# A two-layer hybrid block: where token sums, branch products and expert loads stand in the order of each engine

## The chip, the cores and the metric
One core of a Trainium2 chip runs one launch of the kernel. Five engines take their instructions in their own order: TensorE (PE), VectorE (DVE), ScalarE (ACT), GpSimd (POOL) and SyncE (SP), which here only issues transfers. They meet through semaphores, and 16 DMA engines move data between HBM and SBUF. The metric is the device time of one launch in microseconds (us), the median of the runs.

## The reference, cut to what matters
Per layer, for 128 prompt tokens and 512 sample tokens (640 rows of width 1024, all float32):
```python
h = modulate(rms_norm(x, norm1_g[l]), sh1, sc1)      # sh, sc, g: adaLN, silu(cond) @ w_mod[l] + b_mod[l]
u_f, q_g, k_g, v_g, q_d, k_d, v_d, gates = split(h @ w_in[l])     # q_g and k_g normalised, rope on sample tokens
o_g = gqa_attention(q_g, k_g, v_g)                   # 8 heads, 2 kv heads
o_d = diff_attention(q_d, k_d, v_d, diff_lambda[l], ...)          # 4 heads, softmax minus lambda * softmax
g_f, g_g, g_d = split(sigmoid(gates), 3)
merged = g_f * (fourier_mix(u_f) @ w_f) + g_g * (o_g @ w_go) + g_d * (o_d @ w_do)
x = x + g1 * (merged @ w_out[l])
h = modulate(rms_norm(x, norm2_g[l]), sh2, sc2)
x = x + g2 * moe(h, ...)     # 16 experts in 4 groups, 2 of the best group for each token
```
There are two layers; a last rms_norm gives the outputs, and the new keys and values are returned too.

## The kernel before, in words
**Precision.** A float32 product is made of three fast ones: each operand is split into a high part, rounded by a copy, and a low part, the difference. `mm_split` (matmuls at L181) does high x high, high x low and low x high. So every 1 MB chunk of weights needs a high part from ACT (`hi`, L897) and a low part from POOL (`lo`, L817) or DVE (`first_lo`, L1220; L1299) before TensorE can use it. Activations lie with features on partitions: `x_T`, `h_hi`, `h_lo`, 8 blocks of 128 features by 640 tokens.

**Start of layer 1.** SP loads four 2 MB blocks of the modulation weights and the first two chunks of w_in (`stream`, L720). TensorE turns x to `x_T`, does the modulation products (`mod_product(0..3)`, L1594), spreads the norm's factors over the partitions (`spread_rstd`), turns the gains (`row_in`) and the modulation (`turn_mod`, L1583). DVE copies the norm's factors, computes the low part of the first weights (L1220, 27.47), the first scaled block, the gains, and the multiplier `mul1`; then ACT modulates (L151), DVE and POOL split `h` (L163, L166, L174), and TensorE begins with the first chunk's products (`project`, L181). Its second half of features waits for modulation blocks 2 and 3. When its first modulations are done ACT issues eight small loads (L212 to L214, L908 to L912), the last of them `lam_in`, from diff_lambda (L912). DVE's next step (L1274) needs it, and behind that on DVE stand the folded inputs of the Fourier part (L1290 to L1293) that TensorE reads at L1698.

**Projections.** SP loads the DFT tables, rope and caches, then chunk after chunk into two buffers (`raw`, `stream(i)`). Behind `stream(4)` it stores `x_T` to HBM (`x_kept`, L752), since its room is used later; semaphore `x_moved` tells POOL. TensorE does for each chunk five token tiles ("z" units) and turns the normed and roped tiles back ("x" units). Four PSUM banks go round; ACT empties them (L1016, L1034) and DVE does norm and rope (L1335 to L1374).

**Token sums.** The gate and merge products use fewer multiplications through sums of blocks (a Strassen-like scheme): four token-side sums s_1 to s_4 of `h`, and weight-side sums of blocks of each chunk (`block_sum`, L1481, on DVE; `block_hi`, L1060, on ACT; `block_lo`, L874, on POOL, all 128x512). In the order of POOL, five token-wide adds (L833, 128x1280) stand behind its last low part of a chunk, so they run at the start of the attention. ACT makes the high parts (`sum_high(0)`, `sum_high(1)`, L1047) at items 12 and 13 of the attention, and POOL then the low ones (L855). The third sum follows the attention: three adds, then `sum_high(2)` on ACT ahead of the block parts, and POOL's low part (L863). DVE adds up the fourth (L1488 to L1491) after the first block sums.

**Attention.** `att` lists the items, one head of one token tile each. For each: scores (L1684), maximum (L1380), exponential (L977), division (L1392, DVE), turning and values (L1776). In layer 1 TensorE also does the rest of the modulation products; in layer 2 gate products.

**Merge.** The branch products (`branch(n)`, with `pw_hi` and `pw_lo`, L1096 and L1452) and the remaining gates in blocks (L1509 adds their parts), then the output products with w_out. Counter `g_pfree` counts the branch weights that are used up, and `o_full` (1 to 8) the finished output blocks. In layer 2 the program's order is branch(0), branch(1), branch(2), ... with the blocks between them, and DVE's first block sums come before `mg_sum` (L1536) of the first branch.

**MoE.** SP issues four expert loads of 512 KB (L1974) at `g_pfree` 24, and the other twenty of the first tile (L1980, L1966) once all output products are done and the last low part of the weights is read. The router's result is worked out on DVE (L2171 to L2316). DVE makes `h_tok` (L2186), and POOL scatters the token rows to HBM in the order of experts with ten indirect transfers (L2034). SP waits for all of them, then loads the sorted rows (`h_sel`, L1988), then issues the loads of the next tile (L1957, L1961). TensorE gathers the first tile's rows by products (L2451), does the first tile (L2422) and turns the next rows (L2410).

## Time and profile before

| | |
|---|---|
| median of 3 runs (lowest, highest) | 1942.72 us (1937.16, 1942.76) |
| profiled execution; its span | 1943.26 us; 1941.2 us |
| busy: PE, DVE, ACT, POOL | 1726.5, 957.3, 718.6, 501.9 us |
| mean granted TensorE clock | 0.957 |
| layer 1: start and projections, attention, merge, MoE | to 217, 400, 709, 990 us |
| layer 2: the same | to 1185, 1349, 1650, 1941 us |

The stage ends are read from the timelines. "Busy" counts the time in which an engine executes; a granted clock of 1.00 is 2.4 GHz and of 0.50 is 1.2 GHz. In a timeline's row stand the start, the length, the engine, the line of the program and the tiles written and read; in brackets stands how long the engine was idle before, and what released it. A queue is q1 for SP's and q10 for ACT's transfers, q0 for POOL's.

### The profile page before, as it was taken

What the parts mean: (1) busy time and instruction counts of PE and PEld (TensorE: products, weight loads), DVE (VectorE), ACT (ScalarE), POOL (GpSimd) and SP (SyncE); (2) the same over time, 40 slices, a digit from 0 to 9 for tenths busy, and PEclk for the clock granted to TensorE, in tenths of its full rate; (3) what the DMA queues carried; (4) which work ended last, traced back from release to release, by engine and by line L of the source; (5) the groups of instructions that cost most, each with busy time, mean ns of one, the idle gap of its engine ahead of it and who ended that gap; (6) DMA issues with size and microseconds to landing.
All of it is one profiled execution on the core that took longest, in us unless ns stands there. A gap on an engine that the chain in (4) does not pass through costs nothing. (4 is left out here: it accounts for less than half of the span.)

```text
span 1941.2 us, 34689 instructions
## 1 busy us (share of the span) xinstructions
PE 1726.5 (89%) x13363; PEld 1351.5 (70%) x13363; DVE 957.3 (49%) x1849; ACT 718.6 (37%) x1394; POOL 501.9 (26%) x268
## 2 busy tenths in 40 slices
PE   5999999989999987788689998888899999588893
PEld 4899866679999974222188997567899998432222
DVE  4285476785667333111283744766766652611114
ACT  4443465553433421111254434656433342211113
POOL 1303410065456302000101123201545551200004
PEclk8999999999999988999789999999999999899996
DMA  7512377823522337987442221001232340889744
GB/s 275 195 44 68 106 249 248 275 94 129 192 91 88 143 143 298 360 303 261 143 147 98 67 67 36 1 2 44 66 98 66 98 145 21 354 311 393 278 136 174
DMA packets 170647, 305.95 MB, mean 158 GB/s; under 512 B 12530, under 2 KB 123250, under 8 KB 169716
## 3 DMA queue, kind: packets, MB, share of 16 engines
q1 hardware_dynamic: 151248, 249.09, 37.1%
q10 hardware_dynamic: 13476, 33.67, 4.8%
q0 software_dynamic: 5760, 20.97, 2.9%
q8 instruction: 107, 1.75, 0.4%
q14 instruction: 56, 0.46, 0.1%
HBM read 517.87 MB, written 41.68 MB: 288 GB/s over the span
## 5 line engine op out<-in xcount | busy, mean ns | idle before, releaser
L2422 PE MATMUL psum<-xw,h_T 128*32 128x512 f32 x1792 | 209.3, 611 | 36.0 <-DMA xw<-w_expert 32.4
L181 PE MATMUL psum<-whi,h_hi 128*128 128x256 f32 x720 | 210.1, 292 | 0.5 <-ACT v_tok L1011 0.5
L817 POOL TENSOR_TENSOR wlo<-raw,whi 128x2048 fp32r<-128x2048 f32 x25 | 115.2, 4608 | 362.3 <-ACT whi L897 362.3
L181 PE MATMUL psum<-whi,h_lo 128*128 128x256 f32 x720 | 203.5, 283 | 0.0
L181 PE MATMUL psum<-wlo,h_hi 128*128 128x256 f32 x720 | 203.5, 283 | 0.0
L2422 PEld LDWEIGHTS psum<-xw,h_T 128*32 128x32 f32 x1792 | 53.9, 111 | 170.5 <-issue 113.5
L977 ACT ACTIVATE prob<-psum,small_stats 128x640 f32<-128x640 f32 (+1 forms) x160 | 112.0, 705 | 134.5 <-DVE small_stats L1380 134.3
L1380 DVE TENSOR_REDUCE small_stats<-psum 128x1 f32<-128x640 f32 (+1 forms) x160 | 107.3, 712 | 96.7 <-PE psum L1684 72.2
L2319 DVE TENSOR_TENSOR gated_x<-psum,sig_x 128x256 f32<-128x256 f32 x28 | 11.9, 425 | 279.9 <-ACT sig_x L2066 279.9
L181 PEld LDWEIGHTS psum<-whi,h_hi 128*128 128x128 f32 x720 | 137.5, 191 | 3.0 <-issue 1.8
L181 PEld LDWEIGHTS psum<-wlo,h_hi 128*128 128x128 f32 x720 | 137.9, 192 | 0.0
L181 PEld LDWEIGHTS psum<-whi,h_lo 128*128 128x128 f32 x720 | 137.6, 191 | 0.0
L874 POOL TENSOR_TENSOR weight_block_lo<-weight_block_sum,weight_block_hi 128x512 fp32r<-128x512 f32 x84 | 116.3, 1416 | 79.8 <-DVE weight_block_sum L1481 63.3
L2041 POOL DMA_INDIRECT y_ab<-y_rows,rows_ab x20 | 23.0, 1150 | 431.4 <-DMA y_rows<-y_sel 425.9
L2435 PE MATMUL psum<-xw,act_T 128*32 128x512 f32 x896 | 110.7, 630 | 21.2 <-DMA xw<-w_expert 11.5
L874 POOL TENSOR_TENSOR weight_block_lo<-raw,weight_block_hi 128x512 fp32r<-128x512 f32 x63 | 105.2, 1683 | 74.1 <-ACT weight_block_hi L1060 74.1
L181 PE MATMUL psum<-h_hi,weight_block_hi 128*128 128x320 f32 x336 | 103.8, 309 | 0.0
L181 PE MATMUL psum<-h_lo,weight_block_hi 128*128 128x320 f32 x336 | 103.8, 309 | 0.0
L181 PE MATMUL psum<-h_hi,weight_block_lo 128*128 128x320 f32 x336 | 103.8, 309 | 0.0
L1684 PE MATMUL psum<-k_T,q_T 64*128 64x320 f32 x512 | 86.2, 455 | 14.8 <-ACT prob L977 14.2
L2435 PEld LDWEIGHTS psum<-xw,act_T 128*32 128x32 f32 x896 | 29.0, 115 | 96.5 <-issue 69.7
L181 PE MATMUL psum<-branch_hi,pw_hi 128*128 128x320 f32 x384 | 88.9, 313 | 4.6 <-DVE pw_lo L1452 4.6
(375 smaller groups left out, 4108.3 us busy)
## 6 DMA issues: line engine op xcount, KB each, us to landing
xw<-w_expert SPq DMA_DIRECT2D x672, 512.0 KB
raw<-w_in SPq DMA_DIRECT2D x46, 1024.0 KB, 5.4
wm_rest<-w_mod SPq DMA_DIRECT2D x40, 1024.0 KB, 5.3
y_rows<-y_sel ACTq DMA_DIRECT2D x108, 128.0 KB, 5.2
h_sel<-h_rows ACTq DMA_DIRECT2D x22, 512.0 KB, 6.9
wm<-w_mod SPq DMA_DIRECT2D x4, 2048.0 KB, 16.1
raw<-w_out SPq DMA_DIRECT2D x8, 1024.0 KB, 5.2
h_rows<-c_zero ACTq DMA_DIRECT2D x4, 1536.0 KB, 8.9
```

Source lines behind the costliest of these rows:

```text
L181: mm = pe.matmul(dst, st, mv[q], start=start and n == 0, stop=stop and n == 2)
L817: pool.tensor_tensor(wlo[i % 2][:, :, :], raw[i % 2][:, :, :], whi[i % 2][:, :, :].bitcast(F32), ALU.subtract).then_inc(w_lo, 1)
L874: pool.tensor_tensor(dst, src, w_ring[0][:, slot, :, :].bitcast(F32), ALU.subtract).then_inc(w_lo, 1)
L977: act.activation(dst, scores_view(i, m), ACT.Exp, bias=small[:, s, 0:1], accum_out=small[:, s, 1:2]).then_inc(t_exp, 1)
L1380: dve.tensor_reduce(small[:, 2 * (i % 3) + m, 0:1], scores_view(i, m), AX.X if att[i][2] == 0 else AX.XY, ALU.max, negate=True).then_inc(t ...
L1684: mm = pe.matmul(pair(m)[:, hf, 0:HALF], q_slice(i, m), k_slice(i, m, hf * HALF, (hf + 1) * HALF), start=True, stop=True)
L2041: pool.indirect_dma_start(out=y_ab[t][:, s, :], out_offset=None, in_=y_rows, in_offset=bass.IndirectOffsetOnAxis(ap=pos_ab[:, s, t:t + 1], ...
L2319: dve.tensor_tensor(gated_x[:, :], psum[:, i % 2, 0:DE], sig_x[:, :], ALU.mult).then_inc(x_gt, 1)
L2422: mm = pe.matmul(psum[list_rows(q), i % 2, :], hT[i % 2][:, kc, q, :], xw[q][c][:, k * 512:(k + 1) * 512], start=(kc == 0), stop=(kc == KD ...
L2435: mm = pe.matmul(psum[list_rows(q), 5 + hf, :], aT[i % 2][:, j, list_rows(q)], xw[q][N_PARTS + hf][:, j * 512:(j + 1) * 512], start=(j == ...
```

## The change
It moves steps within the orders of the engines; the mathematics and the matmuls stay.
- Start of layer 1: the spread norm and the turned gains come before `mod_product(1)`; the low part of chunk 0 comes behind `mul1` on DVE; ACT's high part of chunk 1 comes behind the first modulation; `mod_product` and `turn_mod` of blocks 2 and 3 take other places between the projections.
- `x_kept` is stored behind `stream(2)`, in both layers.
- POOL's five adds come behind its low part of chunk 3, and the low parts of s_1 and s_2 behind that of chunk 6; ACT's high parts of both come before two z units of chunk 5.
- Merge of layer 1: `sum_high(2)` comes behind the first two block parts. Layer 2: POOL's third sum waits for the end of the turned differential outputs, `sum_high(2)` comes behind all seven block parts, DVE's first block sums behind `mg_sum` of the second branch, and s_4's low part behind the fourth.
- MoE: seven expert loads instead of four at `g_pfree` 24, four more at `o_full` 6, and the others as before.
```diff
-                        if i == 4:
+                        if i == 2:
                             if first:
                                 sp.wait_ge(s_xe, KD)
                             sp.dma_start(x_kept, x_T[:, :, :]).then_inc(x_moved, 16)
...
                         lo(i)
+                        if i == CH_KVG - 1:
+                            first_sums()
+                        if i == CH_QD + 1:
+                            for n, s in enumerate((s_1, s_2)):
+                                pool.wait_ge(a_hi, n + 1)
+                                pool.tensor_tensor(s[1], (f_1, f_2)[n][1], f32(s[0]), ALU.subtract).then_inc(a_lo, 1)
+
+                    if not first:
+                        pool.wait_ge(d_3, DH)
                     pool.wait_ge(t_o, NA)
...
-                        hi(1)
...
                             modulate_act(act, h_mix, mul1, shift1, kc)
+                        if first and kc == 0:
+                            hi(1)
...
+                        if u in (("z", CH_QD, 1), ("z", CH_QD, 3)):
+                            sum_high(u[2] // 2)
...
-                        if i in (12, 13):
-                            sum_high(i - 12)
...
-                        sum_high(2)
                         pw_high(1)
                     else:
                         pw_high(0)
-                        sum_high(2)
...
                     keep_diff()
-                    for j in range(2, 7):
-                        block_hi(n0, j)
+                    if first:
+                        sum_high(2)
+                        for j in range(2, 7):
+                            block_hi(n0, j)
+                    else:
+                        for j in range(2, 7):
+                            block_hi(n0, j)
+                        sum_high(2)
...
-                        first_lo(dve, 0)
...
                         scaled_gain(mul1, 8, 0, 0, 4).then_inc(m_done, 1)
-                    else:
-                        pass
+                        first_lo(dve, 0)
...
-                            if g == 0:
+                            if not first and g == 1:
+                                first_blocks()
+                            if g == (0 if first else 3):
                                 dve.wait_ge(a_hi, 4)
...
                         mod_product(0)
-                        mod_product(1)
                         spread_rstd(pe)
                         pe.wait_ge(s_row, 16 * 3 * DEPTH)
                         pe.transpose(psum[:, 4, 0:P], row_in[:, :], ident[:, :]).then_inc(m_rt, 1)
+                        mod_product(1)
...
-                            if kc < 2:
-                                mod_product(2 + kc)
-                            if 1 <= kc < 3:
-                                turn_mod(1 + kc)
+                            if kc % 2 == 0:
+                                mod_product(2 + kc // 2)
+                            else:
+                                turn_mod(2 + kc // 2)
...
                     sp.wait_ge(g_pfree, 24)
-                    for c in range(N_PARTS):
-                        sp.dma_start(xw[0][c][:, :], w_exp[c, 0]).then_inc(xw_ld[c], 16)
+                    EARLY = [(c, 0) for c in range(N_PARTS + 1)] + [(2, 3), (3, 3)]
+                    LAST_STREAM = [(0, 2), (1, 2), (2, 1), (3, 1)]
+                    for c, q in EARLY:
+                        first_part(c, q)
+                    sp.wait_ge(o_full, KD - 2)
+                    for c, q in LAST_STREAM:
+                        first_part(c, q)
                     sp.wait_ge(o_full, KD)
```
`first_sums` holds the five adds of L833 with the waits that they had (`n_lo`, `x_moved`), `first_blocks` the block sums and the three steps of s_4 (L1488 to L1491), and `first_part(c, q)` one expert load of 512 KB. Behind the last line the loads of the first tile that are in neither list follow.

## Rows read from the trace of the kernel before

**Rows 1.** The page, part 4: the chain that ended last, by line.
```profile
PE psum L181 22%; SPq L1957 2%; PE psum L1684 2%; DMA xw<-w_expert 2%; ACT prob L977 2%; PE psum L2422 1%; PE psum L2435 1%; DVE small_stats L1380 1%; SPq L1961 1%; SPq L1953 1%; PE psum L1716 1%; PE psum L1749 1%; DVE prob L1392 1%; POOL h_rows L2034 1%; PE psum L1776 0%
```

**Rows 2.** Timeline of DVE in layer 1's start: start, us, what, [idle before <-releaser].
```profile
27.47 2.29 DVE L1220 TENSOR_TENSOR wlo<-raw,whi 128x2048 fp32r<-128x2048 f32 x1 [0.80 <-ACT whi L897]
...
67.60 0.29 DVE L1274 TENSOR_TENSOR lam_pr<-lam_in 128x128 f32<-128x128 f32 x1 [9.95 <-DMA lam_in<-diff_lambda]
...
97.05 0.42 DVE L1335 TENSOR_REDUCE z_ss<-z_q 128x4 f32<-128x256 f32 x1 [22.79 <-ACT z_q L1022]
```

**Rows 3.** Timeline of TensorE in layer 1's start.
```profile
34.07 0.87 PE L181 MATMUL psum<-h_hi,whi 128*128 128x320 f32 x2 [6.54 <-DVE h_lo L166]
...
70.57 0.67 PE L1698 MATMUL psum<-dft_ch,u_T 128*128 128x256 f32 x2 [0.27 <-DVE u_middle L1293]
```

**Rows 4.** Timeline of the issuing queues, ACT's and SP's, in layer 1's start.
```profile
60.47 0.86 ACTq L912 DMA_DIRECT2D lam_in<-diff_lambda  x1
...
56.10 1.40 SPq L720 DMA_DIRECT2D raw<-w_in  x2
```

**Rows 5.** DMA views of 63.5 to 67 (second line: queue) and 87 to 92.
```profile
q10 hardware_dynamic: 517, 0.15, 18.9%
...
DMA packets 122, 2.14 MB, mean 429 GB/s; under 512 B 4, under 2 KB 18, under 8 KB 18
```

**Rows 6.** Windows of five attention items: us, busy (x) by engine, PEclk, DMA share, GB/s.
```profile
1203.30:1227.19 23.89, 17.95 (x165) 13.06 (x163) 20.16 (x30) 12.23 (x26) 15.70 (x6) 0.93 0.01 1
1247.83:1267.60 19.77, 16.53 (x164) 12.04 (x162) 12.80 (x30) 12.22 (x26) 0.00 (x0) 1.00 0.00 1
247.78:269.30 21.52, 21.39 (x246) 14.13 (x242) 14.53 (x35) 12.29 (x25) 0.00 (x0) 1.00 0.76 244
269.30:291.70 22.40, 21.91 (x251) 14.65 (x247) 17.15 (x36) 14.54 (x27) 5.83 (x2) 1.00 0.74 243
```

**Rows 7.** Timeline of POOL, in layer 1's projections and layer 2's attention.
```profile
82.05 4.52 POOL L817 TENSOR_TENSOR wlo<-raw,whi 128x2048 fp32r<-128x2048 f32 x1 [0.91 <-ACT whi L897]
...
1210.15 2.89 POOL L833 TENSOR_TENSOR h_sum_second_f<-h_sum_second_f,h_sum_first_f 128x1280 f32<-128x1280 f32 x1
```

**Rows 8.** Timeline of DVE in layer 2's attention.
```profile
1211.92 4.56 DVE L1392 TENSOR_SCALAR prob<-prob,small_stats 128x640 f32<-128x640 f32 x2
...
1224.65 1.02 DVE L1392 TENSOR_SCALAR prob<-prob,small_stats 128x640 f32<-128x640 f32 x2
```

**Rows 9.** Window in layer 1's projections; columns as in rows 6.
```profile
108.00:124.00 16.00, 16.00 (x137) 16.00 (x136) 13.59 (x39) 8.21 (x23) 0.00 (x0) 1.00 0.22 68
```

**Rows 10.** Timeline of ACT, in layer 1's projections and merge.
```profile
127.65 0.36 ACT L1034 ACTIVATE q_T<-psum 128x256 f32<-128x256 f32 x1
...
412.28 1.26 ACT L1047 ACTIVATE h_sum_hi<-h_sum_second_f 128x1280 fp32r<-128x1280 f32 x1
```

**Rows 11.** Timeline of TensorE: projections, MoE of layer 1, merge and MoE of layer 2.
```profile
129.42 0.36 PE L181 MATMUL psum<-whi,h_hi 128*128 128x256 f32 x1
...
755.90 1.97 PE L2410 MATMUL psum<-ident,h_sel 128*128 128x128 f32 x8 [5.62 <-DMA h_sel<-h_rows]
...
1380.78 0.90 PE L181 MATMUL psum<-branch_hi,pw_hi 128*128 128x320 f32 x2 [4.60 <-DVE pw_lo L1452]
...
1697.35 1.97 PE L2410 MATMUL psum<-ident,h_sel 128*128 128x128 f32 x8 [5.95 <-DMA h_sel<-h_rows]
```

**Rows 12.** Windows: the lower clock in layer 2's merge, and the output products.
```profile
1379.90:1386.70 6.80, 5.92 (x22) 5.92 (x23) 4.04 (x3) 0.86 (x1) 4.44 (x2) 0.50 0.17 31
1606.00:1650.00 44.00, 44.00 (x297) 38.38 (x295) 10.03 (x22) 8.32 (x14) 5.80 (x2) 1.00 0.00 1
```

**Rows 13.** DMA queues from 1672 to 1694: packets, MB, share of 16 engines.
```profile
q0 software_dynamic: 1440, 5.24, 58.5%
q1 hardware_dynamic: 792, 2.85, 32.3%
```

**Rows 14.** The chain that ended last, 1640 to 1760, in order of time.
```profile
1684.96 8.55 DMA h_rows<-h_tok,rows_ab
```

More of the change, by code:

```diff
@@ L822, in _ @@
                             modulate_pool(pool, h_mix, kc)
-                    for i in range(2, N_WIN + n0):
-                        if i in (CH_KVG, CH_QD):
-                            continue
-                        lo(i)
                     n_step = [0]
@@ L1481, in block_sum, with first_blocks @@
                         dve.tensor_tensor(out, x, y, ALU.subtract).then_inc(q_sum, 1)
-                    for m in range(4):
-                        block_sum(n0, m)
-                    dve.wait_ge(a_step, SUM_STEPS)
                     s4_hi, s4_lo = f_4
-                    dve.wait_ge(a_lo, 2)
-                    dve.tensor_tensor(s4_lo, h_12[0].bitcast(F32), s_2[0].bitcast(F32), ALU.subtract).then_inc(a_step, 1)
-                    dve.tensor_tensor(s4_hi, h_12[1].bitcast(F32), s_2[1].bitcast(F32), ALU.subtract).then_inc(a_step, 1)
-                    dve.wait_ge(a_step, SUM_STEPS + 2)
-                    dve.tensor_tensor(s4_lo, s4_lo, s4_hi, ALU.add).then_inc(a_step, 1)
+                    def first_blocks():
+                        for m in range(4):
+                            block_sum(n0, m)
+                        dve.wait_ge(a_step, SUM_STEPS)
+                        dve.wait_ge(a_lo, 2)
+                        dve.tensor_tensor(s4_lo, h_12[0].bitcast(F32), s_2[0].bitcast(F32), ALU.subtract).then_inc(a_step, 1)
+                        dve.tensor_tensor(s4_hi, h_12[1].bitcast(F32), s_2[1].bitcast(F32), ALU.subtract).then_inc(a_step, 1)
+                        dve.wait_ge(a_step, SUM_STEPS + 2)
+                        dve.tensor_tensor(s4_lo, s4_lo, s4_hi, ALU.add).then_inc(a_step, 1)
+                    if first:
+                        first_blocks()
                     n_acc = 0
@@ L1962, in load_down @@
                                      bounds_check="skip_entire_dma").then_inc(xd_ld[h], 16)
-                    def first_down(q):
-                        for h in range(2):
-                            sp.dma_start(xw[q][N_PARTS + h][:, :], w_exp[N_PARTS + h, PER_LIST * q]).then_inc(xd_ld[h], 16)
                     def store_y(i, lists):
@@ L1977, in _ @@
                     low_ready(sp, N_STREAM - 1)
-                    for c in range(N_PARTS):
-                        for q in range(1, N_LISTS):
-                            sp.dma_start(xw[q][c][:, :], w_exp[c, PER_LIST * q]).then_inc(xw_ld[c], 16)
-                    for q in (0, 1, 3):
-                        first_down(q)
+                    rest = [(c, q) for c in range(N_PARTS) for q in range(N_LISTS)] + [(N_PARTS + h, q) for q in (0, 1, 3) for h in range(2)]
+                    for c, q in rest:
+                        if (c, q) not in EARLY + LAST_STREAM:
+                            first_part(c, q)
                     sp.wait_ge(k_d, TT)
-                    first_down(2)
+                    for h in range(2):
+                        first_part(N_PARTS + h, 2)
                     sp.wait_ge(k_t, KD)
```

42 lines of the change are left out of this document (22 added, 20 removed).

## The prediction
> **What bounds the kernel now.** I read the chain that ended last first [rows 1]: by line, the split products of TensorE (L181) hold the largest part, and two causes stand in the MoE, the loads of expert weights and POOL's scatter of the token rows (L2034). So TensorE's own time is the floor nearly everywhere, and the change moves no matmul away: it can gain only where TensorE waits or where the clock is down, and it loses wherever a moved step makes TensorE wait. I then took the six places that the diff touches, one by one, in the timelines of their engines and in windows. All times are of the profiled execution, 1943.26 us around a span of 1941.2; the median of the three runs is 0.5 lower, so I subtract the same gain from 1942.72.
>
> **1. Start of layer 1.** DVE's low part of the first weights, 2.29 us at 27.47 [rows 2], stands ahead of the gains and the first scaled rows; behind it comes the row that ends TensorE's wait of 6.54 us at 34.07 [rows 3]. Taken out of that path it gives some 2.0 us, as the spread norm and the turned gains come before the second product of the modulation vector. But what TensorE reaches next is not its own to start early: at 70.57 it waits for DVE [rows 3], and DVE stands at 67.60 after 9.95 us of waiting for the load of diff_lambda [rows 2], which ACT issues at 60.47, behind its scalings [rows 4]. ACT's last scalings are released by the last mod turn, which with the new order I put 0.25 us later, not sooner, so the 2.0 us are spent in front of 70.57. I take +0.3 us (0 to 1; it would be -2.0 if the load were already there, and the row says it is not).
>
> **2. The store of x_T (L752) is issued behind stream 2 instead of stream 4.** Nothing on an engine waits for it but POOL's sums. It does lie in SP's queue in front of stream 3 and beside ACT's small loads. Stream 2 (issued in the pair at 56.10 [rows 4]) is through near 63.5, and at that point 517 packets of the ACT queue are still to come [rows 5]: about 32 for each of 16 engines. Now the store follows. Its packets show from 87 to 92: 122 packets make 2.14 MB, 20 KB for nearly every one, at 429 GB/s [rows 5]; the 2.6 MB of x_T take 6.1 us. If the engines take packets of the two queues in turn, each of the next 8 small packets of an engine stands behind 20 KB, and the other 24 wait till the store is through. diff_lambda then lands about 5.4 us later, at 73.0, and TensorE starts its next stage at 76.0 instead of 70.57. A wait of this length lowered the clock in the merge of layer 2, and 2.7 us were lost by it (part 5 has its rows); this stage has short gaps of its own anyway, so I take a quarter, 0.7, on top of the 5.4. Part 2 costs 6.1 us, with ends 0 (the small packets slip through) and 8.1 (5.4 and 2.7). In layer 2 the small loads are issued when the store is long through: 0. A sentence for the rule: the Trainium skill, page "DMA: Bandwidth & Descriptors", says that the queues share the 16 engines; how two queues with packets of unlike size take turns is what this kernel's rows leave open, and by an even share of packets the sum stands as above.
>
> **3. Token sums leave the attention.** POOL's five adds (2.9 us each) and two low parts run beside the first scores. The adds hold DVE up: two normalisations took 4.56 us at 1211.92, beside the adds (POOL, 2.89 us at 1210.15 [rows 7], the next right behind), and 1.02 at 1224.65 with POOL idle [rows 8]. The pace, by equal groups of five items: in layer 2 the first takes 23.89 us and one with POOL idle 19.77 [rows 6], a gain of 4.1 from the adds. In layer 1 the group with the two low parts takes 22.40 against 21.52 [rows 6]: 0.9, and the same again in layer 2. For layer 1's adds, where the loads and TensorE's extra products already hold the pace, 0.4. Together 4.1 + 0.9 + 0.9 + 0.4 = 6.3 us gained (4 to 8). Beside it, the Trainium skill ("SBUF — State Buffer", the part on the port pair that DVE and GpSimd share) says that the pair is locked for a whole instruction; the trace agrees, with 4.56 against 1.02.
>
> **4. The same work in the projections.** There it meets DVE again: the adds now start after the fourth low part, at 86.6 in layer 1 (82.05 plus 4.52 [rows 7]) and at the like place in layer 2, and run 15.1 us, to 101.7. DVE's first row of the norms starts at 97.05 [rows 2]; its first two-input step is at 98.7. That step is blocked to the end of the adds: 3.0 us late. DVE has 2.4 us to spare in 16 (13.59 busy [rows 9]), so it hardly catches up before the tightest place, where ACT frees a bank at 128.0 (127.65 plus 0.36 [rows 10]) and TensorE needs it at 129.42 [rows 11]. So 3.0 - 1.3 (1.4 by these rows, less in the unit behind) = 1.7 us of TensorE's time per layer, -3.3 in all (0 if the delay is absorbed before; 8 if the two low parts, 2.9 us each, near 147 and 1103, come on top).
>
> **5. Merges.** In layer 1 the high part of the third sum leaves ACT's 412.28 [rows 10] for about 423.6, and POOL's low part and its seven block parts queue behind it. TensorE needs the first block near 430: -0.4 us (0 to -2). In layer 2 the branch products come first: the wait of 4.60 us [rows 11] on DVE's low part goes, and with it the half clock from 1379.9 to 1386.7, in which 5.92 us of work ran at 0.50 [rows 12], 0.53 us for a pair that takes 0.29 later: 2.7 us. That is 7.3 us at most. But the block sums now begin after the second branch and the third sum's high part (1.26 [rows 10]) and low part (2.9 to 3.6) behind six block parts. I place the branches' end at 1382.5 and the first block product at 1387: a new wait of 4.5 us, with a lower clock again. Late next is POOL, not DVE. Net +1.0 us (0 to 3.5).
>
> **6. Expert weights.** Eleven of the first 24 loads, not four, go out before the last output products end. The DMA engines are idle in that stretch: share 0.00 from 1606 to 1650 [rows 12], so they cost nothing there. Afterwards 7 x 0.5 MB at 410 GB/s are missing, 9 us of a queue that now reaches into the scatter: from 1672 to 1694, q0 (scatter) has 5.24 MB and q1 2.85 MB [rows 13]. POOL issues the last scatter at 1684.96, and it lands 8.55 us later; then SP issues the load of the sorted rows [rows 14], and TensorE's wait for it is 5.95 us in layer 2 and 5.62 in layer 1 [rows 11]. With most of q1's bytes gone the scatter keeps up with POOL's issues (5.24 MB are 12.8 us, the issues take 14.2) and ends about 2.6 us after the last one, near 1688.6: 4.9 us sooner, which leaves a wait of 1.0. Loads of the next tile wait behind the same semaphore on SP, so all that follows moves too. In layer 1 the same gives 3.8. Together +8.7 us (3 to 12).
>
> **Sum:** 6.3 + 8.7 + 1.0 - 3.3 - 0.4 - 0.3 - 6.1 = 5.9 us: 1942.72 - 5.9 = 1936.8 us.
>
> **The rivals.**
> A. **The store does not hold up the small loads.** For it: ACT's packets are tiny, and 517 of them came through in 3.5 us beside another queue. Against it: that queue's packets had 1 KB, not 20. It gives 5.9 + 6.1 = 12.0: 1930.7 us. Chance 0.27.
> B. **The scatter lands no sooner**, as its landing is set by POOL's issues and its own row-by-row writes. For it: the last issue is only at 1684.96. Against it: q0 and q1 together fill the engines to 1692. It takes 8.7 away: 1945.5 us, slower but within the bound. Chance 0.17.
> C. **The lock moves along and decides (the slower side).** Place: DVE's norms and ropes, 13.59 us busy of 16, with TensorE without a gap. If the adds' whole overlap with DVE's rows (4.7 us from 97.05 to the end of the adds) and both low parts (5.8) are lost, less the 1.3 in hand, it is 9.2 per layer, 18.4 instead of 3.3: 1951.9 us. It turns the sign from 4.6 us lost per layer. Against it: single-input steps run beside POOL. Chance 0.10.
> The forecast as summed has 0.42, with its own range 1932 to 1941; 0.04 is for what I have not seen.
>
> **The numbers.** About 0.3% (5.8 us) can be told from no change, so faster begins at 1936.9, right at the forecast. Faster: half of 0.42, nearly all of A and a little of the rest, 0.50. Slower: C and the upper part of B, 0.14. Same: 0.36. The range goes from under A's time to B's, 1928 to 1945; C and the far ends are left out.
>
> **What would show it.** Right: DVE's step on diff_lambda at about 73 and TensorE's next stage near 76; five items of layer 2's attention at 19.8 us from the start; a TensorE gap of 1 to 3 us per layer in the projections between 105 and 140; the sorted rows' wait at 1 to 2 us in both layers; a TensorE gap near 1382 before the blocks. Wrong: the load at 67 or below with the store in between (A), the scatter's last landing still 8 us after its issue (B), more than 4.6 us of gaps in each projection stage (C), or a gap that opens where no part of the sum has one.

## The result, and the profile after

The changed kernel takes 1957.51 us (median of 5 runs, 1950.9 to 1965.99) against 1942.72 before: the ratio is 1.0084, with a 95% interval of 1.005 to 1.0119. It is slower by 15 to 16 us, where 5.9 us of gain were forecast. The execution that was profiled took 1965.99 us, 8.5 more than the median. The page of the changed kernel, its part 1 and the chain by line, beside [rows 1]:

```profile
span 1963.7 us, 34690 instructions
PE 1735.6 (88%) x13363; PEld 1352.8 (69%) x13363; DVE 954.4 (49%) x1849; ACT 715.3 (36%) x1394; POOL 509.8 (26%) x268
PE psum L181 16%; ACT prob L984 2%; SPq L1974 2%; PE psum L1701 2%; DMA xw<-w_expert 2%; PE psum L2444 1%; DVE small_stats L1389 1%; PE psum L2457 1%; SPq L1978 1%; SPq L1970 1%; DVE z_t L1374 1%; POOL h_rows L2056 1%; PE psum L1766 1%; PE psum L1793 0%; DMA h_rows<-h_tok,rows_ab 0%
```

TensorE is busy 9 us longer with the same 13363 instructions (1735.6 against 1726.5 us), and the chain runs less through its products (L181) than before, 16% against 22%. The stages show where the time went. Each column is one profiled execution; a row is the time from one instruction to another that every kernel has, read from the timelines (the "router's rows" are ACT's first `x_gained` of a layer, the "gather of the results" is POOL's first indirect load of `y_ab`). (The last five columns are experiments of the next section: the kernel before with the store moved, the changed kernel with one part undone twice, the kernel before with the adds of layer 2 moved, and the kernel before with nothing beside the scatter.)

| stage, us | before | after | store alone | third sum undone | token sums undone | adds in layer 2 | scatter by itself |
|---|---|---|---|---|---|---|---|
| to the first product (L181) | 34.07 | 31.96 | 33.72 | 32.31 | 31.34 | 33.55 | 33.62 |
| to the Fourier stage | 36.50 | 45.76 | 44.09 | 46.00 | 45.17 | 35.80 | 36.93 |
| to the first scores | 142.84 | 148.25 | 145.61 | 147.99 | 144.21 | 142.63 | 142.71 |
| to the first branch product | 209.18 | 208.74 | 210.08 | 208.70 | 209.17 | 209.23 | 209.21 |
| to the router's rows | 228.48 | 236.18 | 228.49 | 228.49 | 236.26 | 228.50 | 228.48 |
| scatter, first issue to load of the sorted rows | 20.53 | 20.66 | 21.75 | 20.96 | 21.99 | 21.58 | 17.72 |
| layer 1: its sorted rows to the gather of the results | 206.86 | 210.52 | 205.93 | 205.50 | 205.83 | 206.95 | 207.74 |
| layer 2: Fourier stage to scores | 142.71 | 146.50 | 142.71 | 146.49 | 142.71 | 144.22 | 142.71 |
| scores to the router's rows | 423.61 | 419.74 | 423.84 | 419.33 | 423.79 | 420.10 | 425.17 |
| scatter, as above | 21.85 | 21.41 | 21.96 | 21.01 | 20.78 | 22.27 | 17.98 |
| layer 2: its sorted rows to the gather of the results | 205.05 | 205.50 | 203.99 | 198.93 | 202.87 | 200.30 | 202.84 |

How far can a row be trusted? The rows of projections and merges come out the same within 0.5 us in kernels that share the code there, so a difference of 1 us in one of them is the edit's. There are two exceptions, and neither is explained: from layer 2's scores to the router's rows the last column has 425.17, and the kernel with the sooner loads alone 425.14, against 423.6 to 423.9 in the others with this code; and the changed kernel with its store behind stream 3 has 417.43 there, against 419.3 to 419.7. Layer 1's attention, to the first branch product, varies by 1.0, so the 0.4 of its gain is not certain. The start varies most. In the five kernels that have the code of before up to there, the Fourier stage begins at 69.35, 70.48, 70.54, 70.57 and 71.31, and in the four with the start and the store of the changed kernel at 76.51, 77.72, 77.82 and 78.31. So the first two rows say nothing about an edit that is worth 1 us. The tiles of the MoE have the same instructions in all of these kernels and take 199 to 205.5 us in layer 2, 203.7 to 210.5 in layer 1; they spread more than any other stage.

By the table the changed kernel is 12.6 us late at the first scores of layer 1, gains 0.4 in that attention, loses 7.7 in layer 1's merge and 3.8 in layer 2's projections, and gets 3.9 back in the rest of layer 2 up to the router's rows.

**Start.** Timelines of the changed kernel: DVE, TensorE, and ACT's issues (beside [rows 2, 3, 4]), then the DMA view of 64 to 68.

```profile
74.75 0.29 DVE L1283 TENSOR_TENSOR lam_pr<-lam_in 128x128 f32<-128x128 f32 x1 [16.19 <-DMA lam_in<-diff_lambda]
...
77.72 0.77 PE L1715 MATMUL psum<-dft_ch,u_T 128*128 128x256 f32 x1 [8.05 <-DVE u_middle L1302]
...
61.08 5.30 ACTq L916 DMA_DIRECT2D sub_raw<-diff_subln_g  x1
66.92 0.58 ACTq L918 DMA_DIRECT2D lam_in<-diff_lambda  x1
```
```profile
q1 hardware_dynamic: 85, 1.72, 99.9%
q10 hardware_dynamic: 85, 0.01, 1.5%
```

diff_lambda arrives at 74.7 instead of 67.6. While the store's packets pass, q1 and q10 move 85 packets each: one for one. q1's are 20 KB (1.72 MB), q10's together 0.01 MB. There is one more thing that I had not foreseen. It stands in ACT's row at 61.08: the issue of a load of 0.5 KB takes 5.30 us (0.92 in the kernel before), by my reading because the queue is full, so that diff_lambda is only issued at 66.92 instead of 60.47. From issue to arrival it then takes 7.8 us, against 7.1 before: nearly the whole delay lies in the issue. The Fourier stage, which ran at full clock before, starts at a granted clock of 0.50:

```profile
77.72:80.72 3.00, 3.00 (x12) 2.82 (x13) 3.00 (x16) 0.25 (x1) 0.00 (x0) 0.50 0.02 5
```

**Projections.** DVE and POOL in layer 2, and TensorE's waits from 1080 to 1196:

```profile
1076.68 2.95 POOL L828 TENSOR_TENSOR h_sum_second_f<-h_sum_second_f,h_lo 128x1280 f32<-128x1280 f32 x1
...
1077.11 2.81 DVE L1350 TENSOR_TENSOR z_s<-z_s,z_i 128x256 f32<-128x256 f32 x1
...
1081.90 0.42 DVE L1350 TENSOR_TENSOR z_s<-z_s,z_i 128x256 f32<-128x256 f32 x1
```
```profile
PE psum L1754 <- DVE z_r L1383: 1.9, 2, 1.2
PE psum L1754 <- ACT q_T L1049: 0.8, 2, 0.4
```

A step of DVE with two inputs takes 2.81 us beside the last of POOL's adds and 0.42 when the adds are over. TensorE waits 0.8 us in two short waits behind the adds, and 1.9 us in two longer ones behind the low parts of s_1 and s_2; in layer 1 it is 0.7 and 1.7 us.

**Merge of layer 1.** Timelines of ACT, POOL and SP (beside [rows 10]), and the waits of TensorE from 540 to 620:

```profile
435.68 1.26 ACT L991 ACTIVATE h_sum_hi<-h_sum_second_f 128x1280 fp32r<-128x1280 f32 x1
...
437.02 4.06 POOL L869 TENSOR_TENSOR h_sum_lo<-h_sum_second_f,h_sum_hi 128x1280 fp32r<-128x1280 f32 x1 [13.77 <-ACT h_sum_hi L991]
441.05 3.50 POOL L880 TENSOR_TENSOR weight_block_lo<-raw,weight_block_hi 128x512 fp32r<-128x512 f32 x2
...
523.83 0.37 SPq L720 DMA_DIRECT2D raw<-w_in  x1
...
546.69 0.37 SPq L720 DMA_DIRECT2D raw<-w_in  x1
...
569.19 0.37 SPq L720 DMA_DIRECT2D raw<-w_in  x1
```
```profile
PE psum L181 <- DVE sig_m L1524: 2.3, 2, 1.3
PE psum L181 <- ACT gate_part_first_third L1162: 2.1, 2, 1.3
```

POOL stands idle for 13.77 us, does the third sum's low part at 437.02 and only then the first block parts, at 441.05; before, they stood at 420.15, which is 432.3 with the 12.1 us of delay so far. For some rounds nothing is lost by it. Then the chunks of the gates are issued 22.9 and 22.5 us apart, where it was 18.4 and 21.3 in the kernel before, and TensorE, which had no gap in this merge before, waits 4.4 us in these rounds, up to 1.3 us at a time. What ends these waits by the profile is ACT's copy of a gate part and DVE's sum `sig_m`, not POOL. Over the whole merge TensorE waits 5.6 us and is busy 2.1 us longer for the same 1561 matmuls.

**Layer 2.** Windows of five items (beside [rows 6]) and TensorE's waits in the merge (beside [rows 11]):

```profile
1231.35:1251.10 19.75, 16.50 (x162) 11.88 (x159) 12.51 (x29) 12.12 (x25) 0.00 (x0) 0.99 0.01 2
1251.10:1270.88 19.78, 16.53 (x164) 12.03 (x162) 12.80 (x30) 12.22 (x26) 0.00 (x0) 1.00 0.00 1
```
```profile
PE psum L181 <- POOL weight_block_lo L880: 5.2, 1, 5.2
```

The attention now runs at 19.8 us for five items in both of these windows, the first of which begins 36 us after the first scores; a window that began 34 us after them took 23.9 before. In the merge a wait of 5.2 us for POOL has taken the place of the 4.60 us for DVE.

**MoE.** The chain of layer 2 (beside [rows 14]):

```profile
1694.26 1.69 POOL h_rows L2056
...
1707.50 8.10 DMA h_rows<-h_tok,rows_ab
1715.67 3.65 DMA h_sel<-h_rows
```

The last scatter lands 8.10 us after its issue begins, where it took 8.55 before.

### The profile page after: what moved, and what is told of

It is laid out like the page before. It is cut to its first block and busy times, and to the rows that moved or that the text cites. A ratio compares the mean times of both kernels' runs of the same rounds, so it can differ in the third digit from the quotient of the medians.

```text
span 1963.7 us, 34690 instructions
## 1 busy us (share of the span) xinstructions
PE 1735.6 (88%) x13363; PEld 1352.8 (69%) x13363; DVE 954.4 (49%) x1849; ACT 715.3 (36%) x1394; POOL 509.8 (26%) x268
## 5 line engine op out<-in xcount | busy, mean ns | idle before, releaser
L2444 PE MATMUL psum<-xw,h_T 128*32 128x512 f32 x1792 | 214.2, 623 | 50.1 <-DMA xw<-w_expert 41.4
L181 PE MATMUL psum<-whi,h_hi 128*128 128x256 f32 x720 | 210.2, 292 | 0.5 <-ACT v_tok L1026 0.5
L181 PE MATMUL psum<-wlo,h_hi 128*128 128x256 f32 x720 | 203.4, 283 | 0.0
L181 PE MATMUL psum<-whi,h_lo 128*128 128x256 f32 x720 | 203.4, 283 | 0.0
L181 PEld LDWEIGHTS psum<-whi,h_hi 128*128 128x128 f32 x720 | 137.5, 191 | 3.5 <-issue 1.8
L181 PEld LDWEIGHTS psum<-wlo,h_hi 128*128 128x128 f32 x720 | 137.9, 191 | 0.0
L181 PEld LDWEIGHTS psum<-whi,h_lo 128*128 128x128 f32 x720 | 137.6, 191 | 0.0
L880 POOL TENSOR_TENSOR weight_block_lo<-raw,weight_block_hi 128x512 fp32r<-128x512 f32 x63 | 112.4, 1800 | 33.1 <-ACT weight_block_hi L1069 33.1
L181 PE MATMUL psum<-h_hi,weight_block_hi 128*128 128x320 f32 x336 | 105.3, 313 | 5.8 <-POOL weight_block_lo L880 5.7
L181 PE MATMUL psum<-h_lo,weight_block_hi 128*128 128x320 f32 x336 | 105.0, 312 | 0.0
L181 PE MATMUL psum<-h_hi,weight_block_lo 128*128 128x320 f32 x336 | 104.9, 312 | 0.0
L828 POOL TENSOR_TENSOR h_sum_second_f<-h_hi 128x1280 f32<-128x1280 f32 x4 | 11.6, 2904 | 330.1 <-DVE mod_rows L1436 175.6
```

Source lines behind the costliest of these rows:

```text
L181: mm = pe.matmul(dst, st, mv[q], start=start and n == 0, stop=stop and n == 2)
L880: pool.tensor_tensor(dst, src, w_ring[0][:, slot, :, :].bitcast(F32), ALU.subtract).then_inc(w_lo, 1)
L2444: mm = pe.matmul(psum[list_rows(q), i % 2, :], hT[i % 2][:, kc, q, :], xw[q][c][:, k * 512:(k + 1) * 512], start=(kc == 0), stop=(kc == KD ...
```

## The experiments

Each experiment gives its median and its ratio to runs of the kernel before on the same chip, with a 95% interval. The stages are read from one profiled execution of each. "Alone" means one part on the kernel before, "undone" one part taken back from the changed kernel.

**The store alone**
```diff
-                        if i == 4:
+                        if i == 2:
```


> The kernel before with one edit: x_T is stored behind stream 2 instead of stream 4. Theory 1 (the store's 20 KB packets hold up ACT's small loads): DVE's step on diff_lambda moves from 67.6 to about 74.5, TensorE's Fourier stage starts at 77 to 78 instead of 70.57, and the whole kernel is 6 to 9 us slower than before. Theory 2 (the later start in the changed kernel comes from the new order of the modulation products and their turns, not from the store): the Fourier stage stays at 70.6 and the time within 1 us.


1948.04 us, ratio 1.0035 (1.0021 to 1.0049). The Fourier stage starts at 77.81 and diff_lambda arrives at 74.8: Theory 1. The stage behind it runs at half clock, in this kernel:

```profile
77.81:83.81 6.00, 6.00 (x24) 5.64 (x25) 3.70 (x18) 1.07 (x2) 0.00 (x0) 0.50 0.01 3
84.00:90.00 6.00, 6.00 (x30) 3.98 (x29) 0.00 (x0) 3.86 (x5) 3.23 (x1) 1.00 0.00 0
```

TensorE works for 6.0 us at 0.50, where half the time would do at full clock, and the stage to the first scores is 2.8 us longer: 10.0 us in all, 7.2 of them up to the Fourier stage. In the changed kernel the clock is back after 4 us. The two kernels that have its start's order and a late Fourier stage, but not the sums in layer 1's projections, need 144.2 us for this stage: 1.4 longer than before, not 2.8.

**The third sum in layer 1, undone**
```diff
                     else:
                         pw_high(0)
+                        sum_high(2)
...
                     if first:
-                        sum_high(2)
                         for j in range(2, 7):
```


> The changed kernel with one edit undone: in layer 1's merge the high part of the third sum stands ahead of the block parts again. Theory 1 (the late third sum puts POOL, the raw buffers and the streams of chunks behind for the whole gate part, so that TensorE waits 1.3 us in several rounds): the merge of layer 1 takes as long as before, 7 to 8 us less than in the changed kernel, and the issues of chunks are 19.4 us apart again. Theory 2 (the rounds are late from the low parts of the branch weights on DVE, whatever POOL's start): the merge gets 2 us shorter at most.


1948.76 us, 1.0053 (1.0032 to 1.0075). The merge takes 228.49 us again, 7.7 less, and TensorE has no gap in it. POOL's steps and SP's issues of chunks in this kernel:

```profile
426.02 3.28 POOL L869 TENSOR_TENSOR h_sum_lo<-h_sum_second_f,h_sum_hi 128x1280 fp32r<-128x1280 f32 x1 [2.47 <-ACT h_sum_hi L991]
432.55 3.07 POOL L880 TENSOR_TENSOR weight_block_lo<-raw,weight_block_hi 128x512 fp32r<-128x512 f32 x2 [3.25 <-ACT weight_block_hi L1069]
...
518.64 0.37 SPq L720 DMA_DIRECT2D raw<-w_in  x1
...
537.01 0.37 SPq L720 DMA_DIRECT2D raw<-w_in  x1
...
558.25 0.37 SPq L720 DMA_DIRECT2D raw<-w_in  x1
```

This is Theory 1, though the issues are 18.4 and 21.2 us apart, as in the kernel before, and not 19.4: one instruction of 1.26 us on ACT, which stands 11 us further back in the changed kernel (435.68 against 424.69), costs 7.7.

**The token sums, undone**
```diff
                         lo(i)
-                        if i == CH_KVG - 1:
-                            first_sums()
...
+                    first_sums()
...
-                        if u in (("z", CH_QD, 1), ("z", CH_QD, 3)):
-                            sum_high(u[2] // 2)
...
+                        if i in (12, 13):
+                            sum_high(i - 12)
```


> The changed kernel with one edit undone: POOL's five adds, both low parts and their high parts are in the attention again. Theory 1 (the port that DVE and POOL share is the price in both places): the projections get 3.5 and 3.8 us shorter, the attentions 0.4 and 3.3 longer, so the whole is 3 to 5 us faster than the changed kernel. Theory 2 (the delay in the projections is carried over from the late start of layer 1 alone): layer 1's projections keep their 3.5 us, and the whole gets 3 us slower, as the attention loses what it gained.


1953.53 us, 1.0067 (1.005 to 1.0084). Against the changed kernel the projections of layer 1, from the Fourier stage to the first scores, are 4.0 us shorter and those of layer 2 3.8, the attention of layer 1 is 0.4 longer and layer 2's rest 4.1. So the sums in the projections lose 3.4 us in all, as Theory 1 has it, and layer 2 rules out Theory 2. (This kernel is a further 1.2 us ahead at the Fourier stage. The adds begin only behind it, at 95.57 in the changed kernel, so this is the spread of the start and not the edit. And its clock is back after 3 us, in the changed kernel after 4, so some 0.5 of the 4.0 may be the clock's.) The branch products first are still in this kernel, and from layer 2's scores to the router's rows it takes 423.79, before 423.61: they are worth nothing there.

**The expert loads, undone**
```diff
...
-                    for c, q in EARLY:
-                        first_part(c, q)
-                    sp.wait_ge(o_full, KD - 2)
-                    for c, q in LAST_STREAM:
-                        first_part(c, q)
+                    for c in range(N_PARTS):
+                        first_part(c, 0)
...
+                        for q in range(1, N_LISTS):
+                            first_part(c, q)
```


> The changed kernel with one edit undone: the expert loads are issued as before. Theory 1 (the scatter lands about 20 us after POOL's first issue, however many loads lie beside it, so early loads give nothing): no more than 2 us either way, the scatter lands 20 to 21 us after its first issue. Theory 2 (early loads gain where they were meant to, and lose it through the late conversion of the gathered rows on ACT): TensorE's wait for the sorted rows is 5 to 6 us again and the wait of 5.40 and 3.28 us ahead of the first tile's products is 1.1 again.


1956.37 us, 1.0077 (1.0061 to 1.0094): the changed kernel's time. The scatter takes 22.70 and 21.88 us, 20.66 and 21.41 with the loads sooner. That is about 1 us, and Theory 1 by size (its 22.70 is past the 21 that it named). As Theory 2 says, the waits of 5.40 and 3.28 us ahead of the first tile are gone; but in the other kernels this wait is 1.1 to 2.8 us, with the sooner loads or without them. In the changed kernel's profile ACT's conversion (L2081) comes 4.32 and 2.20 us behind the last gathering product, elsewhere 1.7 at most. Why is left open.

**The start's order alone** (the two orders on TensorE, `first_lo` on DVE and `hi(1)` on ACT, as in the diff above)

> The kernel before with the new order of layer 1's start alone. Theory 1 (TensorE's first products come 2 us sooner, but the stage behind them waits for the load of diff_lambda, as before): first products at 32, DVE's step on diff_lambda between 67.5 and 68.5, Fourier stage at 70.5 to 71.5, whole kernel within 1.5 us of before. Theory 2 (the sooner start is carried through): Fourier stage at 68.5, 2 us faster.


1939.89 us, 1.0013 (0.9998 to 1.0028). The first products come at 31.36, 2.7 us sooner than before. The Fourier stage, in this kernel's timeline:

```profile
69.25 0.67 PE L1697 MATMUL psum<-dft_ch,u_T 128*128 128x256 f32 x2 [1.04 <-DVE u_middle L1292]
```

diff_lambda is issued at 58.73, 1.7 us sooner than in the profile before, not later as I had it, and the stage starts at 69.25, 1.3 us sooner. But two of the kernels that start as before have 58.65 and 69.35 (the adds alone) and 61.10 and 71.31 (the two loads moved). The three kernels with this order and the old store start the stage at 69.18, 69.25 and 70.03, in the mean 1.0 us before the mean of the five others. That is between the theories and not certain, and the median shows no gain.

**The store behind stream 3, alone and in the changed kernel**
```diff
-                        if i == 4:
+                        if i == 3:
```


> The kernel before with x_T stored behind stream 3 instead of stream 4, that is behind both chunks that are issued at 56. Theory 1 (what hurts is the store lying in the ring while ACT's small loads are on their way): the store's packets start at about 67, when the small loads are done, diff_lambda is in at 67.6 as before, and the time is that of before within 1 us, while the store is through near 74 instead of 94. Theory 2 (any early store hurts, by its bytes or by stream 4 behind it): the Fourier stage is 2 us or more late.

> The changed kernel with x_T stored behind stream 3. Theory 1 (the store alone makes the late Fourier stage of the changed kernel): Fourier stage at 70.5 to 71.5 instead of 77.7, start and Fourier stage together 9 us shorter than in the changed kernel, later stages as there (projections 123.2, merge of layer 1 long), whole 9 us faster than the changed kernel: 1947 to 1949. Theory 2 (the new order of the modulation has its part): it stays 2 us or more above that.


Alone: 1941.82 us, 1.0025 (1.0007 to 1.0043). The Fourier stage starts at 70.16, as Theory 1 says, and projections and attention are those of before. But the time is not within the 1 us of Theory 1, it is some 5 us longer. The profiled execution is the fastest of the ten (1933.4 us) and can't show where; it stays open.

In the changed kernel: 1956.97 us, 1.01 (1.0083 to 1.0116), with the Fourier stage at 76.83. Theory 1 fails here, and by its number Theory 2 holds: with the other order at the start stream 3 has landed at 66.9 instead of 68.3, the store begins while ACT's packets are still on their way, and diff_lambda lands at 73.8. So "behind both chunks" is no safe place.

**What was left, first try** (store behind stream 3, token sums and third sum undone)

> The changed kernel with the store behind stream 3, the token sums in the attention and the third sum's high part ahead of the block parts in layer 1: what is left of the change is the start's order, the branch products first in layer 2, and the sooner expert loads. Theory 1 (by stages: start 0, projections and attention as before, layer 1's merge as before, layer 2's merge 0.6 to 1.0 shorter, MoE 1 to 2 shorter): 1 to 3 us faster than before. Theory 2 (the MoE's tiles take what they are given): within 0.5 us of before.


1943.62 us, 1.0035 (1.0021 to 1.0048): the Fourier stage starts at 76.8, for the same reason. Both theories missed it.

**The adds alone, layer 2 alone** (with that layer's store behind stream 2)
```diff
                         lo(i)
+                        if not first and i == CH_KVG - 1:
+                            first_sums()
+                    if first:
+                        first_sums()
```


> The kernel before with the five adds alone in the projections, in layer 2 only (with its store behind stream 2 there); both low parts stay in the attention. Theory 1 (the lock's price is shared: the adds cost the projections 1.8 us, the low parts the other 1.8, and the adds are what the attention gains from): projections of layer 2 1.5 to 2.2 us longer than before, attention 3.5 to 4.3 shorter, whole 1.5 to 2.5 us faster. Theory 2 (the adds are the whole price in the projections): 3.8 longer there, whole within 0.5.


1937.59 us, 0.9994 (0.9978 to 1.001). Layer 2's projections are 1.5 us longer and its rest 3.5 shorter: a gain of 2.0 us, as Theory 1 has it. So of 3.8 us in layer 2 the adds cost 1.5 and the two low parts 2.3. The median doesn't show the 2.0 us.

**The sooner loads alone** (lists and order as in the diff above)

> The kernel before with the sooner expert loads alone. Theory 1 (the scatter's time, 20.5 to 22 us from POOL's first issue to SP's load of the sorted rows, does not depend on the loads beside it): scatter 0.5 to 1 us shorter in each layer, whole within 2 us of before. Theory 2 (my forecast): scatter 4 to 5 us shorter, whole 8 us faster.


1939.45 us, 1.0001 (0.9986 to 1.0016). The scatter takes 20.89 and 20.61 us: Theory 1.

**Best of the stages** (start's order, branch products first, adds in layer 2)

> What the stages say is worth keeping: the kernel before with the new order of layer 1's start, the branch products first in layer 2, and in layer 2 alone the five adds in the projections; store of layer 1 behind stream 4, loads as before. Theory 1 (stages add up: start 1.3 shorter, layer 2 2 shorter): 2 to 4 us faster than before. Theory 2 (later stages take it back, the MoE's tiles above all): within 1 us.


1936.38 us, 0.9985 (0.9968 to 1.0002): some 3 us faster, likely and not certain. Its stages are 2.7 us shorter in layer 2, and 1.5 up to layer 1's scores, which proves nothing about the start: the kernel with the adds alone has 1.4 there without any edit in layer 1. Theory 1 by its range.

**Nothing beside the scatter** (the sooner loads, and these two moved)
```diff
-                    sp.wait_ge(k_d, TT)
-                    for h in range(2):
-                        first_part(N_PARTS + h, 2)
                     sp.wait_ge(k_t, KD)
                     sp.wait_ge(k_s, 16 * 2 * TT)
                     for i in (1, 2):
                         sp.dma_start(h_sel[i % 2][:, :], h_tiles[i]).then_inc(h_ld[i % 2], 16)
+                    sp.wait_ge(k_d, TT)
+                    for h in range(2):
+                        first_part(N_PARTS + h, 2)
```


> The kernel before with the sooner expert loads, and the two loads that were issued during the scatter moved behind SP's load of the sorted rows, so that nothing lies beside the scatter. Theory 1 (the scatter's end is set by POOL's ten issues, 14.2 us, and a fixed 7 to 8 us behind the last): 20 us or more from first issue to the load of the sorted rows, as with the loads beside it. Theory 2 (transfers beside it hold it up): 17 us, which is the issues and 2.6 us.


1934.59 us, 0.9971 (0.9956 to 0.9987): 5.6 us faster than before by the ratio, 4.6 by the medians. The scatter takes 17.72 and 17.98 us: Theory 2. The queues from 730 to 748, in this kernel and then in the one with the sooner loads alone:

```profile
q0 software_dynamic: 1440, 5.24, 73.3%
```
```profile
q0 software_dynamic: 1234, 4.53, 63.6%
q1 hardware_dynamic: 288, 1.05, 19.9%
```

In the same 18 us the scatter's 1440 packets pass, or 1234 of them beside 288 of the two loads (1.05 MB). In the middle of it, from 738 to 742, the same two kernels move 390 packets and 339, of which the scatter has 129:

```profile
DMA packets 390, 1.40 MB, mean 350 GB/s; under 512 B 48, under 2 KB 48, under 8 KB 390
```
```profile
DMA packets 339, 1.30 MB, mean 326 GB/s; under 512 B 21, under 2 KB 21, under 8 KB 339
q1 hardware_dynamic: 210, 0.79, 63.3%
q0 software_dynamic: 129, 0.52, 31.4%
```

TensorE's wait for the sorted rows, by the view of its waits from 725 to 760, in the same order:

```profile
PE psum L2419 <- DMA h_sel<-h_rows: 2.7, 2, 1.7
```
```profile
PE psum L2419 <- DMA h_sel<-h_rows: 5.0, 1, 5.0
```

**The two loads moved, the rest of the loads as before** (the same edit on the kernel before)

> The kernel before with one edit: the two loads that SP issues during the scatter come behind its load of the sorted rows; the other 22 loads as before, so their last 1.5 to 2 MB still lie beside the scatter's first issues. Theory 1 (only the two in the middle hold it up): 17.7 to 18.3 us from the first issue to the load of the sorted rows, as in x_alone, and the whole 4 to 6 us faster than before. Theory 2 (the bytes at its beginning count as well, so the sooner loads are needed too): 19.5 to 21 us, whole 1 to 3 us faster.


1936.8 us, 0.9995 (0.998 to 1.0011); the scatter takes 19.08 and 19.64 us. This is between the theories: against the 21.8 us of the kernels without any such edit, moving the two loads is worth 2.4 us, and taking away the nearly 2 MB that still lie beside its beginning 1.5 more.

**diff_lambda ahead of the router's loads, with the early store, and in the best version**
```diff
-                    if first:
-                        router_loads(act)
-                    else:
+                    if not first:
                         parts_act()
...
                     act.activation(lam_e[:, :], lam_s[:, :], ACT.Exp).then_inc(m_l, 1)
+                    if first:
+                        router_loads(act)
```


> The kernel before with x_T stored behind stream 2, and ACT's three router loads issued behind the use of diff_lambda instead of ahead of its load. Theory 1 (what counts is how many packets of ACT's queue stand ahead of diff_lambda when the 20 KB packets come, one for one): with 257 packets or more fewer ahead of it diff_lambda lands before 69, the Fourier stage starts at 69 to 71 instead of 77.8, and the whole is 7 to 10 us faster than with the early store alone, 0 to 2 from before. Theory 2 (the store holds up every transfer until it is through): the Fourier stage stays at 76 or later.

> best2 with the router's loads behind the use of diff_lambda. Theory 1 (diff_lambda is what the Fourier stage of layer 1 waits for, 1.04 us in the kernel with the new start's order): Fourier stage at 68.2 to 68.5 instead of 69.2, 1 us faster than best2 and 2 to 4 faster than before. Theory 2 (the folded inputs of DVE behind it are what counts): no gain.


With the early store: 1945.81 us, 1.0024 (1.0003 to 1.0045). diff_lambda at 72.2 instead of 74.8, Fourier stage at 76.57: by the numbers named this is Theory 2's side. Fewer packets ahead bring 2.6 us, and five small loads are still enough to be caught, the last of them issued at 57.40, ahead of the store's first packets. Best version: 1936.79 us, 0.9986 (0.9973 to 0.9999), Fourier stage at 71.2, later than the 69.2 and 70.0 of the two kernels that lack only this: by my reading because ACT now issues three loads (67.49 to 68.99) between the use of diff_lambda and the copies that TensorE waits for. No gain.

**All that gained, together** (best2, the sooner loads, the two loads behind the scatter)

> best2 with the sooner expert loads and the two loads of x_alone behind the scatter. Theory 1 (gains add up: best2 2 to 3 us, x_alone 5.6): 7 to 9 us faster than before. Theory 2 (the tiles of the MoE are bound by their loads and take a part back): 4 to 6 us faster.


1932.46 us (1926.17 to 1936.99), 0.9972 (0.996 to 0.9984): 5.4 us faster than before by the ratio, 4.8 by the medians, and by the two ratios some 22 us faster than the changed kernel. Theory 2: no more than the loads brought alone. It is the fastest version that was run.

## Why the prediction was wrong, step by step

**Step 5, layer 1's merge: the step that failed worst.** I priced the moved high part at 0.4 us, with 2 as the far end, by asking only whether the first block's product would wait. It waits 0.5 us. But POOL's seven block parts, the release of the raw buffers and the next chunk's load all stand behind it, and there the lateness stays. It measured 7.7 us, shown by undoing this edit alone. How it travels from POOL at 441 to the waits near 549, 568 and 589 is only my reading: the chain of load, high parts, sums on DVE and low parts on POOL is nearly as long as a round of TensorE's work, and the branch products of these rounds share ACT and DVE with it.

**Step 2, the store: right mechanism, size off.** The turns by packet are as forecast (85 for 85), and rival A has fallen. The term was 6.1 us and is 10.0 with the store alone: 7.2 up to the Fourier stage instead of 5.4, as one issue on ACT takes 6.72 us in that kernel, and 2.8 instead of 0.7 for the lower clock. In the changed kernel, together with the start's order, it is 8.5: 7.1 and 1.4. The start spreads by some 1 us either way, and these numbers with it.

**Step 4, the projections: right mechanism, and one term left at nothing.** They cost 4.0 and 3.8 us against 1.7 each; I had named 8 for both as the far end and took 3.3. The two low parts, which I had left at nothing, are the larger part: with the adds alone layer 2 loses 1.5, which is my 1.7, and the low parts cost the other 2.3. The adds meet DVE's rows for 4.3 us in both layers (4.7 in my sum), so the late start of layer 1 makes no difference there. Rival C had the place right, but not the size: it gave 9.2 per layer.

**Step 3, the attention:** it gained 3.9 us in layer 2 (with the merge's 0) and 0.4 in layer 1, against 5.0 and 1.3. The pace is as forecast. The sums cost DVE time wherever they stand. The Trainium skill ("SBUF — State Buffer", section "Who interferes with whom") says that the port pair which DVE and GpSimd share is an exclusive lock for the whole instruction. The trace agrees in both stages: 4.56 us against 1.02 in the attention, 2.81 against 0.42 in the projections.

**Step 6, the loads: the second that failed.** Rival B was right: the scatter lands 0.8 us a layer sooner (kernels without the sooner loads: 21.8 us in the mean of 18 scatters, with them and nothing else moved 21.0 in 12), not 4.9 and 3.8, and the median of the kernel with the sooner loads alone shows nothing of it. Rival B's reason was wrong: alone, the scatter takes 17.7 to 18.0 us, near the 16.9 that I gave it. What I had overlooked is which loads the change takes away. Those in the middle of the scatter are the two that wait for `k_d`, and the change leaves them there. The three kernels show both parts: 21 us with the sooner loads, 19.1 to 19.6 with the two loads moved, 17.7 to 18.0 with both. One sign that I had named for this step did come, by luck: TensorE waits 1.48 us for the sorted rows in layer 2 and not at all in layer 1, but mostly because the first tile begins 2.20 and 4.32 us late there and takes 8.77 and 9.39 us instead of 7.07.

**Step 5, layer 2, and step 1:** +1.0 was forecast for the branch products, and it is 0: the new wait for POOL came as described, 5.2 us long instead of 4.5. (With the adds in layer 2's projections the rest of layer 2 takes 420.1 us without the branch products first and 419.4 to 419.7 with them in three kernels: at most 0.7, near the spread of this row.) The start's order was to cost 0.3 and gives perhaps 1.0 up to the Fourier stage by itself, within the spread of the start; in the changed kernel the wait for diff_lambda swallows it.

With the measured terms the forecast's sum is 4.3 - 7.8 - 7.7 - 8.5 = -19.7 us: attention, projections, layer 1's merge, and the store together with the start's order. The spans of the two profiled executions differ by 22.5; most of the rest is 3.7 us in the tiles of layer 1's MoE, which spread by 6.8 in kernels with the same instructions. By medians and ratio the loss is 15 to 16.

## What to carry to other kernels

An instruction that moves back in a periodic pipeline can be paid in later rounds and not in the first: count the slack of the round, not of its first product. A large store behind a load is not free when another queue's small packets are on their way: here each of them waited for a packet of 20 KB. Before a difference of 1 us in one stage is called an edit's, look how far that stage spreads in kernels with the same code there. Before counting bytes that leave a busy stretch, look up which transfers lie in it, and which event issues them.

## What the runs showed that I had not expected

- Two loads of 0.5 MB in the middle of the scatter lengthen it by about the time of their bytes or a little more: by 3.2 and 2.6 us in the two layers (20.89 and 20.61 against 17.72 and 17.98), where 1.05 MB at 410 GB/s are 2.6. In the 4 us in which they pass, the scatter gets 129 of 339 packets, and 339 are fewer than the 390 that it moves alone.
- An issue on ACT can stand for 5.30 us, and for 6.72 with the store alone, with no wait of the program in it. A full queue is my reading; it was not tried by itself.
- The tiles of the MoE take 199 to 205.5 us in layer 2 and 203.7 to 210.5 in layer 1 with the same instructions. A gain of 2 us ahead of them is seen in the stages and not in the median. A scatter that is 3.9 us shorter per layer is seen in the ratio (0.9971), one that is 2.4 shorter is not (0.9995).
